# Dilated attention with its near group on blocks of consecutive tokens, and the input in natural order

## What is computed

```
DILATED_GROUPS = ((128, 1), (512, 4), (2048, 16))
for gi, (win, dil) in enumerate(DILATED_GROUPS):
    q, k, v = (to_residue(qkv[:, :, gi, j], dil) for j in range(3))
    o, lse = banded_attention(q, k, v, slopes, dil, win // (2 * dil), BLOCK_B)
    outs.append(from_residue(o)); lses.append(from_residue(lse))
wts = softmax(stack(lses), axis=0)
o = einsum('gbsh,gbshd->bshd', wts, stack(outs))
x = x + o.reshape(b, s, 1024) @ w_out
```

## Time and profile before

| | us |
|---|---|
| median of 3 runs | 2229.49 (2227.95 to 2229.78) |
| span of the profiled execution | 2229.6 |
| TensorE busy in it | 2195.3 |
| VectorE, ScalarE, GpSimd busy | 1011.5, 831.7, 734.9 |
| attention units with projection blocks | 629.2 to 1081.5 |
| last four units, with pieces of the output projection | 1081.5 to 1131.6 |

### The profile page before, as it was taken

One profiled execution on the slowest core, in us unless ns is written; L12 is line 12 of the kernel. 1 busy time (PEld: TensorE's weight loads), 2 busy tenths in 40 slices (PEclk: granted clock), 3 DMA queues, 4 the chain that ended last, 5 costly groups with the idle time before them and its releaser, 6 DMA issues.

```text
span 2229.6 us, 31455 instructions
## 1 busy us (share of the span) xinstructions
PE 2195.3 (98%) x13194; PEld 1787.4 (80%) x13194; DVE 1011.5 (45%) x1531; ACT 831.7 (37%) x1291; POOL 734.9 (33%) x339
## 2 busy tenths in 40 slices
PE   9999999999999999999999999999999999999999
PEld 7778888888889888898778888887886667877677
DVE  5665555531223232322356555444504674552672
ACT  6544333333234343443443333233314532333531
POOL 3116444455433332233154444442330101233102
PEclk9999999999999999999999999999999999999999
DMA  4113444432322222222124444423211000322002
GB/s 149 39 38 115 146 146 142 142 113 95 116 86 67 67 71 72 67 67 67 48 76 142 143 146 148 149 95 102 67 57 52 1 1 30 107 76 90 1 1 76
DMA packets 54588, 190.30 MB, mean 85 GB/s; under 512 B 7088, under 2 KB 8368, under 8 KB 54064
## 3 DMA queue, kind: packets, MB, share of 16 engines
q1 hardware_dynamic: 43056, 153.72, 21.1%
q10 hardware_dynamic: 11392, 34.57, 4.2%
HBM read 186.16 MB, written 2.10 MB: 84 GB/s over the span
## 4 chain that ended last, share of the span: by engine, by line
PE 86%; DVE 4%; ACT 1%; issue 1%; DVEq 1%; POOL 0%; ACTq 0%; POOLq 0%
PE ps L174 21%; PE ps L176 21%; PE ps L175 20%; PE ps L2560 4%; PE ps L177 3%; PE ps L179 3%; PE ps L178 3%; PE ps L2592 2%; PE ps L1052 2%; PE ps L1078 2%; PE ps L2572 2%; PE ps L1063 1%; DVE l_h_lo L1632 1%; DVE dvS L1111 0%; PE ps L2116 0%
## 5 line engine op out<-in xcount | busy, mean ns | idle before, releaser
L246 POOL TENSOR_TENSOR w_lo<-w_raw,w_hi 128x1024 fp32r<-128x1024 f32 x282 | 681.8, 2419 | 1391.0 <-ACT w_hi L164 1391.0
L174 PE MATMUL ps<-h_hi,w_hi 128*128 128x512 f32 x1168 | 467.8, 400 | 4.9 <-DVE w_lo L288 2.5
L164 ACT ACTIVATE w_hi<-w_raw 128x1024 fp32r<-128x1024 f32 x284 | 299.4, 1057 | 437.3 <-DMA w_raw<-in_wstream 436.2
L176 PE MATMUL ps<-h_hi,w_lo 128*128 128x512 f32 x1168 | 458.9, 393 | 0.0
L175 PE MATMUL ps<-h_lo,w_hi 128*128 128x512 f32 x1168 | 455.9, 390 | 0.0
L174 PEld LDWEIGHTS ps<-h_hi,w_hi 128*128 128x128 f32 x1168 | 219.4, 188 | 54.2 <-issue 4.0
L176 PEld LDWEIGHTS ps<-h_hi,w_lo 128*128 128x128 f32 x1168 | 219.4, 188 | 48.6
L175 PEld LDWEIGHTS ps<-h_lo,w_hi 128*128 128x128 f32 x1168 | 219.5, 188 | 46.3 <-issue 0.7
L1255 ACT ACTIVATE sq<-sq,dnm 128x768 f32<-128x768 f32 x64 | 59.5, 930 | 185.3 <-DVE dnm L1161 185.3
L177 PE MATMUL ps<-w_hi,h_hi 128*128 128x256 f32 x416 | 116.9, 281 | 3.2 <-DVE dvS L1111 3.2
L178 PE MATMUL ps<-w_lo,h_hi 128*128 128x256 f32 x416 | 115.3, 277 | 0.0
(11 more groups left out here) (330 smaller groups left out, 4123.5 us busy)
## 6 DMA issues: line engine op xcount, KB each, us to landing
w_raw<-in_wstream SPq DMA_DIRECT2D x283, 512.0 KB, 3.5
f0mod_rows<-in_wmod ACTq DMA_DIRECT2D x24, 512.0 KB, 4.5
f1mod_rows<-in_wmod ACTq DMA_DIRECT2D x24, 512.0 KB, 4.1
out<-x SPq DMA_DIRECT2D x8, 256.0 KB, 3.2
x<-in_x SPq DMA_DIRECT2D x3, 512.0 KB, 7.3
l_dft<-in_dft ACTq DMA_DIRECT2D x4, 384.0 KB, 4.4
l_wuq<-in_wuq ACTq DMA_DIRECT2D x2, 768.0 KB, 7.5
dist<-in_dist ACTq DMA_DIRECT2D x1, 1152.0 KB, 5.3
```

The costliest lines, as they stand in the source:

```text
L164: self.A.activation(self.w_hi[:, n % RING, :], self.w_raw[:, n % RING, :], ACT.Copy).then_inc(self.w_high, 1)
L174: T.matmul(out, wh, ah, start=start, stop=False)
L176: return T.matmul(out, wl, ah, start=False, stop=stop)
L246: G.tensor_tensor(c.w_lo[:, n % RING, :], c.w_raw[:, n % RING, :], c.w_hi[:, n % RING, :].bitcast(F32), ALU.subtract).then_inc(c.w_low, 1)
```

## The change

The near group now works on blocks of 128 consecutive tokens. Unit b has as near queries tokens 128b to 128b+127, for which 256 keys do: 64 before, 128 own, 64 behind. The other two groups still take residue b. Near and far parts of one unit thus belong to different queries. So each has an extreme and a sum of its own, the near part's output goes to bank 4 and the far part's to bank 5, and at the end of a tile the two are brought together: VectorE masks the near statistics (`mask_near`), TensorE moves them from token order to residue order with four small products (`exchange`), `invert` takes the common extreme, ScalarE the exponentials (`weigh`), and eight transposes (two times four) spread the two factors; `norm_out` multiplies each part and adds. A tile's chain is placed at the start of the next tile's first unit.

h stays in natural order. Keys and queries of groups 1 and 2 (counted from 0) are put in residue order by VectorE as it evacuates them; their values are made with the stationary operand read with a step of four (`slice(t, SEQ, DIL)`). The near values are also kept a second time, shifted by 64 rows (`vE`), since a block of keys starts half a block earlier or ends half a block later.

The unit's order changes: scores of the unit come before its dense blocks (up to three in a row), then its transposes, then the values of the unit before. Bias tables are made once a tile. `da_out` uses four banks (6, 7, 0, 1) and an order of pieces of its own (`late`). Some semaphores of the later layers are shared, which moves no instruction of theirs.

```diff
-    segments = []
-    for i in range(3):
-        a, b = qk(2 * i + 1), qk(2 * i + 2)
-        vs = v(i + 1, 0) + v(i + 1, 1) + v(i + 1, 2)
-        segments += [a[0:2], a[2:3], a[3:4], a[4:5], a[5:6], vs[0:1], vs[1:2], vs[2:3]]
-        segments += [vs[3:4], vs[4:5], vs[5:6], b[0:2], b[2:3], b[3:4], b[4:5], b[5:6]]
-    a = qk(7)
-    segments += [a[0:1], a[1:2], a[2:3], a[3:4], a[4:5], [], a[5:6], []] + 8 * [[]]
-    return first, segments
+    a, b = qk(1), qk(2)
+    steps = [a[0:3], a[3:6], v(1, 0), v(1, 1), b[0:3], b[3:6], v(1, 2)]
+    a, b = qk(3), qk(4)
+    steps += [a[0:3], a[3:6], v(2, 0), v(2, 1), b[0:2], b[2:5], b[5:6], v(2, 2)]
+    a, b, last = qk(5), qk(6), qk(7)
+    steps += [a[0:3], a[3:6], v(3, 0), v(3, 1), b[0:2], b[2:5], b[5:6], v(3, 2)[0:1]]
+    steps += [v(3, 2)[1:2] + last[0:1], last[1:3], last[3:4], last[4:5], last[5:6]] + 4 * [[]]
+    return first, steps
...
+        if late:
+            pairs = [(m, k) for b in (0, 2) for k0, k1 in ((0, 6), (6, 7)) for m in (b, b + 1) for k in range(k0, k1)]
+            self.left[0:len(pairs)] = pairs
+        self.split_ahead = int(late)
...
+            if b >= self.split_ahead:
+                c.split_high(self.n0 + b + LEAD)
...
+    def by_block(ap):
+
+        return ap.rearrange("p (i r) -> p r i", r=DIL)
+
+    @staticmethod
+    def by_residue(ap):
+
+        return ap.rearrange("p (r i) -> p r i", r=DIL)
...
-                ts = slice(t * P, (t + 1) * P)
                 for k in range(4):
                     kk = 4 * half + k
-
-                    ins = c.mm3(c.flat(bank, t * 256, 256), wh[:, k, :], wl[:, k, :], self.h[0][:, kk, ts],
-                                self.h[1][:, kk, ts], kk == 0 and t % 2 == 0, kk == KT - 1 and t % 2 == 1,
-                                w_is_lhs=False, shared=True)
+                    tok = slice(t * P, (t + 1) * P) if g == 0 else slice(t, SEQ, DIL)
+                    ins = c.mm3(c.flat(bank, t * 256, 256), wh[:, k, :], wl[:, k, :], self.h[0][:, kk, tok], self.h[1][:, kk, tok],
+                                kk == 0 and t % 2 == 0, kk == KT - 1 and t % 2 == 1, w_is_lhs=False, shared=True)
...
-                    ins = T.transpose(c.ps[:, 4, t * P:(t + 1) * P], c.RB[:, t * P:(t + 1) * P], c.ident[:, :])
+                    T.transpose(c.ps[:, 4, t * P:(t + 1) * P], c.RB[:, t:SEQ:DIL], c.ident[:, :])
+                for t in range(TT):
+                    ins = T.transpose(c.ps[:, 5, t * P:(t + 1) * P], c.RB[:, t * P:(t + 1) * P], c.ident[:, :])
...
+            tile = u // 4 - 1
+            between = u % 4 == 0 and u
+            self.scores(u)
+            if between:
+                self.exchange(tile)
+            for i, b in enumerate(self.steps[u]):
                 self.dense(n, b)
                 n += 1
+                if between and i == 0:
+                    self.spread_over_rows(tile)
             if u == 28:
                 T.wait_ge(self.evacuated, len(self.chunks))
-                T.wait_ge(self.spread_out, 7)
-            if u >= 28:
+                out.pieces(5)
+                self.spread_over_rows(tile)
+            if u > 28:
                 out.pieces(3)
             self.turn_probs(u)
-            for b in self.segments[2 * u + 1]:
-                self.dense(n, b)
-                n += 1
-            if u >= 28:
-                out.pieces(2 if u < 31 else 1)
-            if u % 4 == 3:
-                self.spread_over_rows(u // 4)
-            self.sum_values(u)
-            if u + 1 < self.UNITS:
-                self.scores(u + 1)
-
-    @staticmethod
-    def pieces(u):
-
-        return [(0, t) for t in range(DIL)] + [(1, u % 4), (2, u % 4)]
+            if u:
+                self.sum_values(u - 1)
+        T.wait_ge(self.biased, 4 * self.UNITS)
+        out.pieces(2)
+        self.exchange(7)
+        self.sum_values(self.UNITS - 1)
+        out.pieces(5)
+        self.spread_over_rows(7)
+        out.pieces(7)
...
+            T.wait_ge(self.biased, 4 * u)
+        near = [(0, r * P, 3 * HD) if r < 3 else (HD, r * P - HD, 3 * HD)]
+        if r in (1, 2):
+            near.append((3 * HD, r * P - HD, HD))
+        pieces = [(0, at, k0, n) for at, k0, n in near] + [(g, (g + 1) * P, r * P, P) for g in (1, 2)]
+        for g, at, k0, n in pieces:
+            for e in range(2):
+                rows = slice(HD * e, HD * e + HD)
+                ins = T.matmul(c.ps[:, e, at:at + n], self.qT[par][g][rows, r * P:(r + 1) * P],
+                               self.kT[par][g][rows, k0:k0 + n], start=True, stop=True)
+        ins.then_inc(self.scored, 1)
+
+    def turn_probs(self, u):
+
+        c, T, r = self.c, self.c.T, u % 4
+        if u:
             T.wait_ge(self.copied0, u)
             T.wait_ge(self.copied1, u)
-        for i, (g, t) in enumerate(self.pieces(u)):
-            for e in range(2):
-                rows = slice(HD * e, HD * e + HD)
-                ins = T.matmul(c.flat(2 * e, i * P, P), self.qT[par][g][rows, r * P:(r + 1) * P],
-                               self.kT[par][g][rows, t * P:(t + 1) * P], start=True, stop=True)
-        ins.then_inc(self.scored, 1)
-
-    def turn_probs(self, u):
-
-        c, T = self.c, self.c.T
-        T.wait_ge(self.biased, 2 * u + 2)
+        if u >= 4:
+            T.wait_ge(self.spread_out, 2 * (u // 4))
...
+            T.wait_ge(self.exped, 4 * u + 2 * e + 2)
+            for k, at in enumerate(cols):
+                ins = T.transpose(c.ps[:, 2 + e, k * P:(k + 1) * P], self.prob[:, e, at:at + P], c.ident[:, :])
...
+        values = (self.vS[par][0], self.vE[par], self.vS[par][1], self.vS[par][2])
+        for i, value in enumerate(values):
             for e in range(2):
                 col = (tile % 2 * 2 + e) * HD
-                ins = T.matmul(c.ps[HD * e:HD * e + HD, 4, r * P:(r + 1) * P], self.vS[tile // 2 % 2][g][:, t, col:col + HD],
-                               self.probT[:, e, i * P:(i + 1) * P], start=i == 0, stop=i == 5)
+                ins = T.matmul(c.ps[HD * e:HD * e + HD, 4 + i // 2, r * P:(r + 1) * P], value[:, r, col:col + HD],
+                               self.probT[:, e, i * P:(i + 1) * P], start=i % 2 == 0, stop=i % 2 == 1)
...
+    def exchange(self, tile):
+
+        c, T = self.c, self.c.T
+        T.wait_ge(self.near_masked, tile + 1)
+        T.wait_ge(self.copied0, 4 * tile + 4)
+        T.wait_ge(self.copied1, 4 * tile + 4)
+        place = self.dist[:, self.NB + DIL:self.NB + DIL + P]
+        for b in range(TT):
+            ins = T.matmul(c.ps[32 * b:32 * b + 32, 2, 0:16], place[:, 32 * b:32 * b + 32],
+                           self.masked[:, b].rearrange("p r s -> p (r s)"), start=True, stop=True)
+        ins.then_inc(self.exchanged, 1)
...
+        for a in range(2):
+            for r in range(DIL):
+                ins = c.T.transpose(c.ps[:, 3 - a, r * P:(r + 1) * P],
+                                    self.rden[a][:, 2 * r:2 * r + 2, :].rearrange("p e d -> p (e d)"), c.ident[:, :])
+            ins.then_inc(self.spread, 1)
...
+            if g == 0:
+                vE = self.vE[i % 2]
+                V.drain()
+                V.tensor_copy(vE[0:HD, 0:3, :], vS[0:HD, 1:4, :])
+                ins = V.tensor_copy(vE[HD:P, 1:4, :], vS[HD:P, 0:3, :])
...
+            if g:
+                dst, src, r = self.by_residue(dst), self.by_block(src), self.by_block(r)
+            V.tensor_tensor(dst, src, r, ALU.mult).then_inc(self.evacuated, 1)
...
+            if between:
+                self.mask_near(tile)
             self.bias_and_max(u)
-            n += len(self.segments[2 * u])
+            if between:
+                self.invert(tile)
+            if u % 4 == 1 and u > 4:
+                self.low_out(tile)
...
+        V.wait_ge(self.exchanged, tile + 1)
+        V.tensor_tensor(low, other[:, 0], nm, ALU.min)
+        V.drain()
+        V.tensor_tensor(part[:, 0], other[:, 0], low, ALU.subtract)
+        V.tensor_tensor(part[:, 1], nm, low, ALU.subtract).then_inc(self.part_made, 1)
+        V.wait_ge(self.part_exped, tile + 1)
+        V.tensor_tensor(wden[:, 0], other[:, 1], part[:, 0], ALU.mult)
+        V.tensor_tensor(wden[:, 1], den, part[:, 1], ALU.mult)
+        V.drain()
+        V.tensor_tensor(low, wden[:, 0], wden[:, 1], ALU.add)
+        V.drain()
+        V.reciprocal(low, low)
+        V.drain()
+        V.tensor_tensor(part[:, :, :, :], part[:, :, :, :], self.low[:, :, :].unsqueeze(1).broadcast_to([P, 2, DIL, 2]), ALU.mult)
         V.drain()
         if tile:
-            V.wait_ge(self.spread, tile)
-        V.tensor_copy(self.rden[:, :, :], den.unsqueeze(2).broadcast_to([P, 8, HD])).then_inc(self.inverse, 1)
+            V.wait_ge(self.spread, 2 * tile)
+        for a in range(2):
+            ins = V.tensor_copy(self.rden[a][:, :, :], part[:, a].rearrange("p r e -> p (r e)").unsqueeze(2).broadcast_to([P, 8, HD]))
+        ins.then_inc(self.inverse, 1)
...
```

(40 more changed lines are left out.)

213 lines of the change are left out of this document (118 added, 95 removed).

## The result

The changed kernel takes 2305.96 us (median of four runs, 2304.3 to 2307.28), the kernel before 2229.64 in the same session: a ratio of 1.0343, 95% interval 1.0328 to 1.0357. It is 76 us slower. Where a series holds an execution several times as long as its others (6637.77 us once in the first kernel of experiment 4, 12499.94 us once for the kernel before), the ratios leave it out.

A forecast was written before the change was run, and what follows sets the result against it. TensorE, busy 98% of the span, was taken as the bound. From 2229.6 us: units and added small work -40.5, waits +3.5, strided value loads +88.9, strided norm transposes +0.5, giving 2282.0 us; range 2188 to 2297.

The forecast's parts named there:

- A rival that has been priced: Seven tile boundaries become waits: small steps 3 us longer each, 21 us, 2303 with the forecast; no chance of its own.
- the range: The predicted span of the changed kernel's whole time, 2188 to 2297 us, reaching down to the no-cost rival.

The follow-up runs named there:

- the first kernel of experiment 4: The changed kernel with ScalarE's small exponential of a tile boundary moved ahead of the weight split that stood before it: 2299.0 us.

## What to carry to other kernels

Count the 16-byte pieces that a load touches, not its columns; a layout that suits one reader may be paid for by another, and reordering the small product (the values) by a few transfers was cheaper than reading the large input with a step. When a chain of small VectorE operations becomes part of the path, look at what GpSimd is released to do in the same microseconds, and keep its long operation out of the chain rather than shortening the chain. A rival that has been priced belongs inside the range.

## What was new about the hardware

- A TensorE weight load of 128 fp32r columns with 256 moving columns costs 1.84 to 1.91 ns for each 16-byte piece that it touches, once that exceeds what the matmul hides: 0.114, 0.121, 0.1765 and 0.236 us a record at steps of 1, 2, 3 and 4, and 0.245 at 8.
- A VectorE product of eight elements took 2.28 us, and a copy of 512 2.61 us, where GpSimd was in a 2.4 us subtraction; a product that reads one operand from PSUM took 0.17 us beside it.
- One transfer issue of 32 rows took SyncE 0.69 us (11.1 us for 16), one of 128 rows 0.63 us (2.5 us for four): here the number of issues counted, not their bytes.
- A transfer may take 128 rows from 128 partitions and lay them four to a partition.
